# A two-layer recurrent and retention trunk: products of zeros at the start, the first squares summed by VectorE, and the first unit of r moved

## The reference

```
for layer in range(2):
    hn = rms_norm(h, norm_mix_pre[layer])          # h is 512 tokens x 1024
    m = mixer_ab(hn, ...) if layer % 2 == 0 else mixer_ret(hn, ...)
    h = h + rms_norm(m, norm_mix_post[layer])
    f = sq_relu_mlp(rms_norm(h, norm_ffn_pre[layer]), ffn_w_in[layer], ffn_w_out[layer])
    h = h + rms_norm(f, norm_ffn_post[layer])

def rms_norm(x, g, eps=1e-6):
    return x * rsqrt(mean(x * x, axis=-1) + eps) * g

def mixer_ab(h, w_in, w_out, ...):
    u = h @ w_in                                    # ax, ag | r, k, v, dw, da, dg
    ya = rg_lru(causal_conv(ax)) * gelu(ag)
    # mixer B, RWKV-7; every column is mixed with the one of the token before it
    w_log = -softplus(-(w0 + tanh(dw) @ w2)) - 0.5  # low ranks
    a = sigmoid(a0 + da @ a2)
    g = sigmoid(dg) @ g2
    kk = (k * k_k) / norm per head of (k * k_k)
    ... a recurrence over the tokens for 8 heads of 64 ...
    return concatenate([ya, yb]) @ w_out
```

## Time and profile before

| | |
|---|---|
| median of 3 runs | 1519.89 us (1516.77 to 1520.2) |
| the profiled execution, its own time | 1520.04 us |
| span from its first to its last instruction | 1518.3 us |
| PE busy | 1475.6 us (97%) |
| DVE, ACT, POOL busy | 831.6, 504.0, 73.5 us |
| mean granted clock of PE | 0.986 of full speed |

### The profile page before, as it was taken

How to read it: one execution, slowest core, us unless ns; L and a number is a source line. 1 busy time by engine, 2 the same in 40 slices (tenths; PEclk the granted TensorE clock), 3 DMA queues, 4 the chain that set the end, 5 groups by cost and what they waited for, 6 DMA issues and landing times.

```text
span 1518.3 us, 23219 instructions
## 1 busy us (share of the span) xinstructions
PE 1475.6 (97%) x10404; PEld 1232.3 (81%) x10404; DVE 831.6 (55%) x1035; ACT 504.0 (33%) x578; POOL 73.5 (5%) x67
## 2 busy tenths in 40 slices
PE   7999999998999999999899999999998999999998
PEld 5888878786888888888788888888887888888886
DVE  7767585757644445363675455454447635354455
ACT  7444443534322222122343332332434313122222
POOL 1000000002100000000300000000003000000000
PEclk9999999998999999999899999999998999999999
DMA  4202020201322222223032213132131332222322
GB/s 180 71 8 98 3 89 18 84 4 56 125 95 100 92 102 90 105 88 107 28 111 84 83 58 109 57 104 91 56 111 42 112 110 83 93 102 90 105 88 79
DMA packets 19731, 125.62 MB, mean 83 GB/s; under 512 B 2288, under 2 KB 2288, under 8 KB 5808
## 3 DMA queue, kind: packets, MB, share of 16 engines
q1 hardware_dynamic: 19088, 121.23, 23.3%
q0 software_dynamic: 544, 2.91, 0.6%
HBM read 122.03 MB, written 2.10 MB: 82 GB/s over the span
## 4 chain that ended last, share of the span: by engine, by line
PE 88%; DVE 5%; ACT 3%; DMA 1%; POOL 1%; issue 1%; SPq 0%; DVEq 0%; POOLq 0%
PE bank L330 19%; PE bank L336 18%; PE bank L333 18%; PE bank L725 7%; PE bank L534 4%; PE bank L531 4%; PE bank L535 4%; PE bank L1331 2%; PE bank L1334 2%; PE bank L1328 2%; PE bank L344 2%; DVE XL L423 1%; DMA raw<-weights 1%; ACT WH L297 1%; POOL h L462 1%
## 5 line engine op out<-in xcount | busy, mean ns | idle before, releaser
L330 PE MATMUL bank<-XH,WH 128*128 128x512 f32 x944 | 381.6, 404 | 24.6 <-DVE XL L423 12.6
L333 PE MATMUL bank<-XL,WH 128*128 128x512 f32 x944 | 372.0, 394 | 0.0
L336 PE MATMUL bank<-XH,WL 128*128 128x512 f32 x944 | 371.8, 394 | 0.0
L303 DVE TENSOR_TENSOR WL<-raw,WH 128x2048 fp32r<-128x2048 f32 (+1 forms) x111 | 249.8, 2251 | 175.6 <-ACT WH L297 175.5
L297 ACT ACTIVATE WH<-raw 128x2048 fp32r<-128x2048 f32 (+1 forms) x111 | 208.4, 1877 | 277.7 <-DMA raw<-weights 277.7
L330 PEld LDWEIGHTS bank<-XH,WH 128*128 128x128 f32 x944 | 180.3, 191 | 66.6 <-issue 28.7
L333 PEld LDWEIGHTS bank<-XL,WH 128*128 128x128 f32 x944 | 180.5, 191 | 38.7 <-issue 2.6
L336 PEld LDWEIGHTS bank<-XH,WL 128*128 128x128 f32 x944 | 179.9, 191 | 38.9
L647 ACT ACTIVATE AH<-relu 128x512 fp32r<-128x512 f32 x64 | 40.5, 633 | 249.7 <-DVE relu L672 249.7
L330 PE MATMUL bank<-AH,WH 128*128 128x512 f32 x256 | 99.7, 389 | 0.1
L672 DVE SCALAR_TENSOR_TENSOR relu<-bank,rB 128x512 f32<-128x512 f32 x64 | 44.1, 690 | 101.3 <-PE bank L336 101.3
(11 more groups left out here) (298 smaller groups left out, 2054.3 us busy)
## 6 DMA issues: line engine op xcount, KB each, us to landing
raw<-weights SPq DMA_DIRECT2D x107, 1024.0 KB, 4.8
raw<-weights SPq DMA_DIRECT2D x8, 512.0 KB, 5.0
h<-x_fm SPq DMA_DIRECT2D x4, 512.0 KB, 8.0
out_tm<-hT SPq DMA_DIRECT2D x8, 256.0 KB, 2.1
rc<-ret_const POOLq DMA_DIRECT2D x1, 1536.0 KB, 6.8
pp<-pairs POOLq DMA_DIRECT2D x4, 199.0 KB, 5.1
cst<-const SPq DMA_DIRECT2D x1, 577.0 KB, 11.9
gain_row<-last_gain POOLq DMA_DIRECT2D x1, 512.0 KB, 3.5
```

Of the source, the lines that this page charges most:

```text
L303: nc.vector.tensor_tensor(WL[i][:, :n], raw[i][:, :n], WH[i][:, :n], ALU.subtract).then_inc(S("w_lo"), 1)
L330: mm = pe.matmul(bank[b][:], wh, xh, start=(k == 0), stop=False)
L333: mm = pe.matmul(bank[b][:], wh, xl, start=False, stop=False)
L336: mm = pe.matmul(bank[b][:], wl, xh, start=False, stop=(k == len(xs) - 1))
```

## The change

PE gets eleven products of the zeroed tile `rB` with itself into bank 7 ahead of everything else, released by a new memset of `rB` that is POOL's first instruction (`rB` is written with its real values later, by line 419, and bank 7 is cleared by the first product of unit r). The adds of odd tiles move from POOL to DVE, which now does all six adds and the last one. The column sums come behind all eight tiles of the first two units, and tiles 0 to 3 of pair 0's unit r come ahead of the low ranks.

```diff
@@ front_pe, pair 0
                 in_unit(pe, use, "k", 0, (4, KT))
+                in_unit(pe, use, "r", 0, (0, 4))
                 pe.wait_ge(S("lora_ready"), 1)
                 low_ranks()
@@
-            in_unit(pe, use, "r", p, (0, 4))
+            if p:
+                in_unit(pe, use, "r", p, (0, 4))
             need("kk_sq")
@@ gpsimd
+            nc.gpsimd.memset(rB[:], 0.0).then_inc(S("zeros_ready"), 1)
             nc.gpsimd.memset(epsc[:, 0:1], EPS).then_inc(S("eps"), 1)
...
-            pre_sums_pool(pool, 0)
@@ tensor
+            pe.wait_ge(S("zeros_ready"), 1)
+            for _ in range(11):
+                pe.matmul(bank[7][:], rB[:, 0:P], rB[:], start=True, stop=True)
             pe.wait_ge(S("vec_loaded"), 16)
...
-            units(pe, use, [0, 1], first, X, 0, x_tiles(pe, 0), (4, 6))
+            units(pe, use, [0, 1], first, X, 0, x_tiles(pe, 0), (4, KT))
             pre_sums_pe(pe, 0)
-            units(pe, use, [0, 1], first, X, 0, x_tiles(pe, 0), (6, KT))
@@ vector
-            pre_sums_dve(dve, 0)
+            for i in range(3):
+                for k, (total, name) in enumerate(((sum_a, "hsq_sum_a"), (sum_b, "hsq_sum_b"))):
+                    dve.wait_ge(S("hsq"), 2 * i + k + 3)
+                    if i:
+                        dve.wait_ge(S(name), i)
+                    V.tensor_tensor(total, total if i else sq[:, k, :], sq[:, 2 * i + k + 2, :],
+                                    ALU.add).then_inc(S(name), 1)
```

## The result

The changed kernel takes 1520.92 us (median of 22 runs, 1518.74 to 1523.41), the kernel before, measured beside it, 1517.14 us (22 runs, 1514.59 to 1520.92). The ratio is 1.0023, 95% interval 1.0016 to 1.0030: slower by 0.23%, 3.5 us, between 2.4 and 4.6. The size of the change came out as forecast, and 22 runs of each kernel are enough to tell it. The profiled execution took 1520.45 us, its span is 1518.7 us.

A forecast was written before the change was run, and what follows sets the result against it. The prediction took the low ranks' end to bound the stretch up to ax: 2.7 us later ax plus 0.6 us for the clock, 3.3 us on 1520.04, gave 1523.3 us, range 1518.5 to 1527.5.

The forecast's parts named there:

- The end of the low ranks sets ax: First 45 us: unit ax starts 8.87 us behind the low ranks' end (first sigmoid), whatever PE does meanwhile.
- The chain of the prediction: Low ranks release ACT's sigmoids, `kk_sq`, table loads, exponentials; then reciprocal of `kkroot`, DVE's low part of chunk 2, ax.
- Zero products: PE's start: eleven at 0.86 us run from 1.3 to 12.8, delaying real work 2.6 us, which then runs at 2.4 GHz.
- the prediction's estimate by that page: PE's start: 14 cold matmuls give 6.0 us of slow start, ending the zeros at 13.8 instead of 12.8.
- Squares by DVE: DVE's seven adds at 0.69 us without POOL end at 20.5, before PE needs the sum, so cost nothing.
- Sums behind all tiles: Column sums at 23.8 without the 0.69 us wait; k at 25.8, including some 0.6 us waiting; later `lora_ready` harmless.
- Half of r: 12 instructions of r ahead of the low ranks cost 2.75 us; first sigmoid at 35.4, ax 2.7 us later.
- The clock behind it: PE's bare wait for `kk_sq` and two-column products may halve the clock; 0.6 us taken, between nothing and 1.5.
- Rival 1: Half clock reaches ax, slowed r and spread outlast the wait, zeros run slow: 5.7 us loss, 1525.7; chance 0.21.
- Rival 2: Zeros at PE's start do not raise the clock: 9.9 us more, 1533; chance 0.04.
- Rival 3: Zero products take half, 0.43 us each; real work starts at 10.2, ax about 41.6, no change, 1520; chance 0.07.
- Rival 4: Later half-clock stretches shift; three vanishing would give -1.2 us, 1518.8; chance 0.06.

The follow-up runs named there:

- e1: Changed kernel with tiles 0 to 3 of r put back behind the low ranks; ratio 1.0010 to the kernel before, ax at 41.91 us.
- e10: The kernel before once more, unedited; its second profile took 1515.88 us against 1520.04 in the first.
- e4: Kernel before with tiles 0 to 3 of r ahead of the low ranks as only edit; at least 2.9 us slower, ax at 44.18.
- e11: e3 with the root of the key norms and its reciprocal first for pair 0; 1514.08 us, 0.30% below the kernel before.
- e3: Changed kernel with 8 zero products instead of 11 and the half of r back behind the low ranks; ratio 0.9982 to the kernel before.
- e6: Kernel before with only DVE's adds and the column sums behind all eight tiles, no zeros, r in place; ratio 0.9995.
- e2: Changed kernel with 8 zero products instead of 11; time fell by 0.13%, ax at 42.15 us.
- e8: Changed kernel with 22 zero products instead of 11; 0.83% above the kernel before, 12.6 us, ax at 53.73.
- e5: Kernel before with the 11 zero products as its only edit; time that of before, ax at 41.87 us.
- e7: Changed kernel without the zero products and their memset; ratio 1.0003 to the kernel before, ax at 43.59 us.

## Why the prediction was right, point by point

**The end of the low ranks sets ax.** Shown where r stands ahead of them. From the first sigmoid to ax the profiles of before, the changed kernel and e1 to e10 have 8.8 to 9.1 us, although PE is busy for 4.98 us of it in the changed kernel and for 7.64 in before, and in e4 partly at half clock. The distance shortened only in e11, where ACT's own series was cut. The chain of the prediction lacks one link, though. In these twelve profiles ax starts 7.67 or 7.68 us behind ACT's square, and the square needs DVE's mixed keys besides the sigmoids. In the kernel before it starts at 33.90, 0.04 us behind this row:

```profile
33.11 0.75 DVE L1030 SCALAR_TENSOR_TENSOR W<-mixdiff,vec,Uk 128x512 f32<-128x512 f32 x1
```

There the two ends lie together (32.70 + 1.16 = 33.86 by the sigmoids, 33.86 by the keys). In e1, e3 and e6 the keys are the later by 0.2 us, and it is they that set ax; with r ahead of the low ranks they are ready 2.5 us early, and the low ranks alone decide.

**Zero products.** Predicted 1.3 to 12.8 us, measured 1.32 to about 13.1, since the row at 12.71 overlaps the last zero instruction (12.69 + 0.43). The memset took 0.53 us. The 0.3 us is the slow start, 4.6 us long for the 4.0 predicted. Over the eight profiles with zeros it is 3.2 to 5.2 us by the granted clock; the bounds taken were 2.9 and 5.0. The length differs between executions, as the Trainium skill says in "TensorE: Matmul & The Clock Gate", section "What's actually happening". Its 6.0 us, the prediction's estimate by that page, did not occur with zeros; with real products alone e6 had 5.9. Price of one product beyond the eighth: 0.76 us (e2) and 0.85 us (e8), 0.86 predicted; with half the difference of the slow starts put back it is 0.86 in both.

**Squares by DVE.** The adds came every 0.63 us, below the 0.69 used, and the sum came 4 us before it was needed. POOL's absence made them short: two took 3.31 us beside POOL and 3.32 in e5, which keeps POOL's adds.

**Sums behind all tiles.** Predicted start 23.8, k at 25.8; measured 24.03 and 26.01. PE waits 0.66 us for the reciprocal, 0.6 predicted. `lora_ready` came at 30.53, and the low ranks did not wait for it, as predicted. But with r back in place DVE, which mixes the low ranks' input ahead of the keys, starts late by the same later copy to `rB` (26.96 in e1, 26.12 in before): this is the 0.2 us of e1, e3 and e6.

**Half of r.** Predicted to cost 2.75 us. Measured 2.52 (changed less e1), 2.52 (e2 less e3) and 2.61 (e4 less before). With e5 and e6 near zero it is nearly the whole loss of 2.86 us. Below 2.75 it is because, without r ahead, the square waits for the mixed keys: 0.22 us in e1 and e3, 0.04 in the kernel before.

**The clock behind it.** This term was mis-sized. The prediction put 0.6 us for a fall of the clock. It measured 0: in the two profiles of the changed kernel the clock stayed up, and in the three profiles of its relatives in which it fell (e2, e4, e7) the waits behind r took it up. Rival 1 had its condition half met in those three, and its price was not paid at ax in any run. The row on which the term rests was itself a matter of the execution: sixteen one-column products stand between 384 and 402 us in all thirteen profiles, and the fall near 390 followed them in four. The sum at ax without the term is 2.7, measured 2.86 and 3.08. That 3.3 came so near to the measured 3.5 is in part luck: 0.6 us of it did not happen, and about as much between ax and the end of the program has no shown cause.

**Rival 2** (zeros don't raise the clock) is out by the rows of the changed kernel: from the second real product on the starts lie 0.23 us apart. **Rival 3** (a cheaper zero product) is out by e8: eleven more cost 9.3 us. **Rival 4** (later slow stretches shift): they do, but the kernel before does it too, between two of its executions. It is why the two first profiles differ by 0.4 us in span, although ax is 2.86 us later. The medians of 22 runs differ by 3.8 us. Whether the 0.6 us between 2.9 and 3.5 in the middle of the interval are real stays open; so does why e4 and e7, by their intervals, lie 0.3 us outside their ax.

## What to carry to other kernels

Find the step after which both versions run alike, and follow back what releases it; work put ahead of that releaser is paid in full even if the engine is idle later anyway. Work that only warms the clock must end when the real work can begin: here eight ended as the input came, eleven gave back all they had won (no other number between was run), and the best count has to be read from the time at which the last product ends, not from a target for busy time. When two losses hide each other (a slow clock and a late sum), each repair alone measures as nothing, so try them together before dropping either. And before a few tenths of a microsecond between two profiles are put down to an edit, look whether the part ahead of the edit is alike: in e11 0.93 us of 2.50 were not.

## What the runs showed of the hardware

- The same program, unedited, had 17 us of half clock between 355 and 394 us in one profile and 10 us in another, and was 4.2 us shorter in the second (e10).
- Products of zeros raised TensorE's clock as real ones do: the granted clock rose 3.2 to 5.2 us after their start in eight profiles, and 4.5 to 5.9 us after the first real product in the five without zeros.
- Two microseconds without any product, followed by 0.9 us of two-column products, were followed by half clock in e2, e4 and e7 and not in e8 and the changed kernel's two profiles, with the same instructions in the same order in e2, e7, e8 and the changed kernel but for the number of zeros.
- DVE's adds of 128x512 lasted 0.68 us alone and 1.60 us while POOL added beside them (e6 and e5).
